# Differential attention on one Trainium2 core: component scores as three terms on two row halves, row sums later, first-token values by split parts

## The chip, the cores and the metric

The program runs on one NeuronCore of one Trainium2 chip. The metric is the device time in microseconds of one execution. The engines are TensorE (PE, with its weight loads shown as PEld), VectorE (DVE), ScalarE (ACT), GpSimd (POOL) and SyncE (SP), which issues most of the DMAs. PSUM holds eight banks of 512 fp32 columns per partition.

## The reference

A streaming encoder block for 2048 tokens behind 16 first ("meta") tokens, model width 1024. One projection feeds two groups of heads side by side: four heads of differential attention and four of latent attention. Their outputs are mixed, normed, added, and a squared-ReLU MLP follows. The change is in the differential attention:

```python
q1, q2 = q[..., 0, :], q[..., 1, :]          # two components of 64 per head
k1, k2 = k[..., 0, :], k[..., 1, :]
s1 = einsum('bhqd,bhkd->bhqk', q1b, k1) * scale + bias   # bias: distance, chunk mask
s2 = einsum('bhqd,bhkd->bhqk', q2b, k2) * scale + bias
a = softmax(s1) - lam * softmax(s2)
return einsum('bhqk,bhkv->bhqv', a, v)       # v: 128 per head
```

## The kernel before

The kernel runs in stages: entry norm and projections, an upward projection of the latent heads (`mla_up`), differential attention (`attention`), latent attention, mixing, MLP. All engines run their own instruction streams and wait for each other on semaphores. The stage of the change begins with the first score matmul of head 0, and the latent attention's first score matmul follows its end on TensorE, in program order.

**Numbers.** TensorE's single-pass fp32r products are made exact enough by parts: each q and k is stored as a high part and a low part (`scr.qk_hi`, `scr.qk_lo`). Before, the q tile of one component stacks 64 rows of high parts on 64 rows of low parts, and the key tile holds [high; high] and [low; low]. Two matmuls over 128 partitions then give all four terms of a component's scores. The value products (`da_ps_o<-da_pT,da_v`) are plain fp32, each run as two instructions.

**Rows.** A head has 16 row tiles of 128 queries (i = 0 to 15). Row tile i sees 16 + 128(i+1) keys, cut by `row_chunks(i)` into 1 to 5 chunks of up to 512 columns: 44 chunks for a head and component, 17,664 columns, so 88 chunks a head. For each chunk TensorE writes scores to one of four PSUM banks (`da_ps_s`). VectorE (L1535) adds the bias, writes to SBUF and takes the chunk's maximum. After the last chunk of a component it makes the row's negated maximum (L1542). ScalarE does the exponentials with their sum (L1481), the first component in `da_rows`, the second in `da_second`. VectorE inverts the sums (L1567, L1574) and weighs the second with lambda (L1576); GpSimd scales the first component (L1473). VectorE's `end` (L1580) adds the second to the first.

**Turning and products.** Four row tiles make a group g. When its four rows have their sums, TensorE transposes the probabilities tile by tile (`turn`, L1646) into three banks (`da_ps_t`); ScalarE copies each to `da_pT` (L1494). `product` (L1660) multiplies it by the value tile into `da_ps_o`. Tile t = 0 belongs to the first tokens: it transposes the first 128 keys, and `v_meta` has zeros but for 16 rows. Group g has 1 + 4(g+1) tiles, so a head has 44, four of them for first tokens.

**Order.** All engines walk one list, `STEPS`, made by `head_steps` for a steady head. `row_steps` lists the chunks and, some chunks later, each row's `exp`, `scale` and `end`. `PHASES` says which groups' rows go with which groups' turns and products: rows of groups 0 and 1 with the previous head's group 3, rows of group 2 with groups 0 and 1, rows of group 3 with group 2. A phase's third figure says how late in it the turns begin, the fourth how many last steps (products and an `out`) are put off into the next phase. `walk` runs the list for each head; a step marked with `back` 1 belongs to the head before. After the last head, its group 3 and the put-off steps run alone. In head 0, TensorE also makes 12 late products of six matmuls for the latent heads (`late_product`, L1629).

**Loads.** SP loads keys and bias one head ahead, q group by group, values when the previous head has used them.

Of the kernel before, what the change touches and what calls it, by code (L numbers as in the profile page):

```python
# [30 lines left out]
P = 128  # L31
# [1075 lines left out]
def by_component(src, h, cols):  # L1107

    return src[ds(h, 1), :, cols].rearrange("a (c p) n -> p (a c) n", c=2)


def load_q(sp, scr, ahead, h, g):
    for j, src in enumerate((scr.qk_hi, scr.qk_lo)):
        sp.dma_start(f32(ahead.q[64 * j:64 * j + 64, g % 2]),
                     by_component(src, h, slice(META + 512 * g, META + 512 * g + 512))).then_inc(ahead.q_loaded[g % 2], 16)


def load_first_keys(sp, scr, ahead, g):

    c0, n = KEY_PIECES[g]  # L1120
    cols = slice(c0, c0 + n)
    for j, src in enumerate((scr.qk_hi, scr.qk_lo)):
        for half in range(2):
            sp.dma_start(f32(ahead.keys[half * 64:half * 64 + 64, j::2, cols]),
                         by_component(src, DA_H, cols)).then_inc(ahead.start_loaded[g], 16)
# [41 lines left out]
def attention(nc, io, scr, ident, ahead, latent):  # L1167
# [8 lines left out]
    with ExitStack() as ctx:  # L1176
        mem = Memory(nc, ctx, io.used)
        keys = (ahead.keys, mem.sb("da_keys", [P, 4, LP], F32R)[:, :, 0:L])
# [5 lines left out]
        NPT = 8  # L1184
        NTB = 3
        pT = mem.sb(f"da_pT", [P, NPT, 512])
        mx = mem.sb("da_mx", [P, 2, COMPS, 5])
        nmax = mem.sb("da_nmax", [P, 2, COMPS])
        nmax_all = mem.sb("da_nmax_all", [P, 5])
        total = mem.sb("da_total", [P, 2, COMPS])  # L1190
        inv = mem.sb("da_inv", [P, 2, COMPS])
        inv2 = mem.sb("da_inv2", [P, 2])
        lam = mem.sb("da_lam", [P, 4])
        v_meta = mem.sb("da_v_meta", [P, P])
        NSB = 4
# [12 lines left out]
        inv2_step = mem.sem("da_inv2_step")  # L1208
# [9 lines left out]
        chunks = [(i, c, k0, n) for i in range(NT) for c in range(COMPS) for k0, n in row_chunks(i)]  # L1218
# [4 lines left out]
        KEY_LOADS = 4  # L1223
# [9 lines left out]

        def comp_row(i, c, u):
            return row(i, u) if c == 0 else second[:, i % 2, 0:META + P * (i + 1)]

        def row_steps(carried):
# [4 lines left out]
            for groups, *_ in PHASES:  # L1242
                steps = []
                for n, (i, c, k0, w) in enumerate(chunks):
# [6 lines left out]
                    if k0 + w == META + P * (i + 1):  # L1251

                        steps += [step for _, step in later if step[2] - NT * step[1] < i]
                        later = [(left, step) for left, step in later if step[2] - NT * step[1] >= i]
                        later.append((1, ("exp", 0, i, c)))
                        if c == 0:
                            later.append((SCALE_AFTER, ("scale", 0, i)))
                        if c == COMPS - 1:
                            later.append((END_AFTER, ("end", 0, i)))
                phases.append(steps)  # L1260
            return phases, [(left, (step[0], 1) + step[2:]) for left, step in later]

# [4 lines left out]
        def cost(step):  # L1267

            if step[0] == "chunk":
                return chunks[step[2]][3] + 60  # L1270
            return META + P * (step[2] + 1) + 250 if step[0] == "end" else 0

        def head_steps():
# [4 lines left out]
            for p, rows_part in enumerate(row_steps(row_steps([])[1])[0]):  # L1278
# [39 lines left out]
        PHASES = (((0, 1), ((1, 3),), 0.2, 7), ((2,), ((0, 0), (0, 1)), 0.15, 7), ((3,), ((0, 2),), 0.2, 7))  # L1318
        SCALE_AFTER, END_AFTER = 2, 5
# [30 lines left out]
        def slot_free(engine, h, n):  # L1350

            if n >= NPT:
                engine.wait_ge(pv_done, NKT * h + n - NPT + 1)
            elif not (isinstance(h, int) and h == 0):
                engine.wait_ge(pv_done, NKT * (h - 1) + last_user(n, NPT) + 1)
# [8 lines left out]
        def _(sp):  # L1364
            def load_keys(h, u):

                for j, src in enumerate((scr.qk_hi, scr.qk_lo)):
                    for half in range(2):
# [2120 lines left out]
```

## Time and profile before

| | us |
|---|---|
| median of 3 runs | 2591.54 (2589.82 to 2594.27) |
| profiled execution | 2589.82 |
| its span, first to last instruction | 2588.0 |
| differential attention in it | 427.0 to 795.5, 368.5 long |

The profile is of one execution. "Busy" of TensorE counts matmuls whose ends are modelled and which overlap, so the distance from one start to the next says what a matmul costs in a row of them. Times in rows are from the span's start.

### The profile page before, as it was taken

What the parts mean: (1) busy time and instruction counts of PE and PEld (TensorE: products, weight loads), DVE (VectorE), ACT (ScalarE), POOL (GpSimd) and SP (SyncE); (2) the same over time, 40 slices, a digit from 0 to 9 for tenths busy, and PEclk for the clock granted to TensorE, in tenths of its full rate; (3) what the DMA queues carried; (4) which work ended last, traced back from release to release, by engine and by line L of the source; (5) the groups of instructions that cost most, each with busy time, mean ns of one, the idle gap of its engine ahead of it and who ended that gap; (6) DMA issues with size and microseconds to landing.
All of it is one profiled execution on the core that took longest, in us unless ns stands there. A gap on an engine that the chain in (4) does not pass through costs nothing.

```text
span 2588.0 us, 35257 instructions
## 1 busy us (share of the span) xinstructions
PE 2526.3 (98%) x12140; PEld 2103.8 (81%) x12140; DVE 1619.0 (63%) x3515; ACT 1211.9 (47%) x2183; POOL 333.4 (13%) x368
## 2 busy tenths in 40 slices
PE   8999999999999999989999999999999999999998
PEld 7998887677667989868877888888888888888886
DVE  6123307998995777754468777867757465564765
ACT  6112314777765565554544333533335353443554
POOL 2110002222221222110000000000000001121133
PEclk9999999999999999999999999999999999999999
DMA  6324458553333111145677666666655365776787
GB/s 225 131 100 132 119 164 263 139 136 94 88 134 92 34 30 46 42 130 163 195 240 224 208 221 214 220 193 210 189 165 175 118 216 106 174 166 161 201 165 139
DMA packets 328956, 398.35 MB, mean 154 GB/s; under 512 B 20896, under 2 KB 235184, under 8 KB 320464
## 3 DMA queue, kind: packets, MB, share of 16 engines
q1 hardware_dynamic: 311216, 364.17, 44.8%
q0 software_dynamic: 17568, 31.99, 8.5%
q8 instruction: 95, 1.56, 0.3%
q14 instruction: 77, 0.63, 0.1%
HBM read 239.62 MB, written 156.48 MB: 153 GB/s over the span
## 4 chain that ended last, share of the span: by engine, by line
PE 62%; DVE 3%; DMA 1%; ACT 1%; issue 1%; SPq 0%; POOL 0%; DVEq 0%; ACTq 0%; POOLq 0%
PE ff_ps_x L3277 26%; PE ff_ps_m L3277 13%; PE ff_ps_z L3277 6%; PE ml_ps_s L2153 6%; PE ff_ps_m L1702 4%; PE ml_ps_o L2184 3%; PE ml_ps_t L2166 2%; DMA ml_v_raw<-scr_yT 1%; DMA ff_pieces<-scr_acc 0%; PE ff_ps_r L2714 0%; PE mo_ps_t L2731 0%; SPq L2341 0%; PE ml_ps_o L2180 0%; DVE ff_pieces L2444 0%; DMA work<-scr_w_vo 0%
## 5 line engine op out<-in xcount | busy, mean ns | idle before, releaser
L3277 PE MATMUL ff_ps_x<-ff_mv_hi_p,ff_st_hi_p 128*128 128x512 f32 x764 | 297.8, 390 | 0.5 <-ACT ff_u L3017 0.5
L3277 PE MATMUL ff_ps_x<-ff_mv_lo_p,ff_st_hi_p 128*128 128x512 f32 x764 | 297.3, 389 | 0.0
L3277 PE MATMUL ff_ps_x<-ff_mv_hi_p,ff_st_lo_p 128*128 128x512 f32 x764 | 297.2, 389 | 0.0
L2153 PE MATMUL ml_ps_s<-wide,ml_qs 128*128 128x416 f32 (+14 forms) x880 | 197.0, 358 | 3.0 <-PEq L137 2.8
L3123 DVE TENSOR_TENSOR ff_st_lo_p<-ff_ps_m,ff_st_hi_p 128x512 fp32r<-128x512 f32 x190 | 130.5, 688 | 103.4 <-ACT ff_st_hi_p L3000 103.4
L2967 POOL DMA_DIRECT2D scr_acc<-ff_pieces x64 | 55.5, 872 | 1015.3 <-DVE ff_pieces L3147 946.8
L3017 ACT ACTIVATE ff_u<-ff_ps_x 128x512 f32<-128x512 f32 x128 | 76.6, 598 | 214.9 <-PE ff_ps_x L3277 214.9
L3277 PEld LDWEIGHTS ff_ps_x<-ff_mv_hi_p,ff_st_hi_p 128*128 128x128 f32 x764 | 143.4, 188 | 32.4 <-issue 2.0
L3277 PEld LDWEIGHTS ff_ps_x<-ff_mv_hi_p,ff_st_lo_p 128*128 128x128 f32 x764 | 143.4, 188 | 29.9
L3277 PEld LDWEIGHTS ff_ps_x<-ff_mv_lo_p,ff_st_hi_p 128*128 128x128 f32 x764 | 143.4, 188 | 29.5
L2153 PEld LDWEIGHTS ml_ps_s<-wide,ml_qs 128*128 128x128 f32 x880 | 153.4, 193 | 15.3 <-issue 3.4
L3000 ACT ACTIVATE ff_st_hi_p<-st_raw 128x512 fp32r<-128x512 f32 x191 | 119.4, 626 | 86.3 <-PE ff_ps_z L3277 86.3
L3277 PE MATMUL ff_ps_m<-wide,ff_st_hi_p 128*128 128x512 f32 x512 | 157.7, 389 | 0.4 <-DVE ff_st_lo_p L2618 0.4
L3000 ACT ACTIVATE ff_st_hi_p<-ff_ps_m 128x512 fp32r<-128x512 f32 x190 | 113.2, 598 | 93.7 <-PE ff_ps_m L3277 93.7
L3277 PE MATMUL ff_ps_x<-wide,ff_st_hi_p 128*128 128x512 f32 x504 | 155.1, 389 | 0.0
L3123 DVE TENSOR_TENSOR ff_st_lo_p<-st_raw,ff_st_hi_p 128x512 fp32r<-128x512 f32 x191 | 130.8, 687 | 36.9 <-ACT ff_st_hi_p L3000 35.6
L2062 DVE CUSTOM_DVE_ANT_0 ml_rows<-ml_ps_s,ahead_bias 128x416 f32<-128x416 f32 (+14 forms) x176 | 100.1, 569 | 67.8 <-PE ml_ps_s L2153 59.8
L1660 PE MATMUL da_ps_o<-da_pT,da_v 128*128 128x512 f32 (+3 forms) x320 | 137.2, 529 | 0.0
L1985 ACT ACTIVATE ml_pT_hi<-ml_ps_t 128x512 fp32r<-128x512 f32 (+3 forms) x176 | 90.6, 537 | 88.6 <-PE ml_ps_t L2166 88.5
L1613 PE MATMUL da_ps_s<-da_keys,ahead_q 128*128 128x416 f32 (+14 forms) x352 | 112.6, 423 | 2.4 <-DVE da_mx L1535 2.4
L3277 PEld LDWEIGHTS ff_ps_m<-wide,ff_st_hi_p 128*128 128x128 f32 x512 | 96.0, 188 | 20.5 <-issue 0.6
L3277 PEld LDWEIGHTS ff_ps_x<-wide,ff_st_hi_p 128*128 128x128 f32 x504 | 94.6, 188 | 19.6
(322 smaller groups left out, 6326.1 us busy)
## 6 DMA issues: line engine op xcount, KB each, us to landing
st_raw<-in_w_ff SPq DMA_DIRECT2D x64, 512.0 KB, 6.1
scr_hid<-ff_pieces SPq DMA_DIRECT2D x128, 256.0 KB, 2.7
st_raw<-scr_hid SPq DMA_DIRECT2D x64, 512.0 KB, 5.6
ring<-in_w_ff SPq DMA_DIRECT2D x28, 1024.0 KB, 8.0
scr_t<-ring SPq DMA_DIRECT2D x24, 1024.0 KB, 6.0
ring<-scr_t SPq DMA_DIRECT2D x21, 1024.0 KB, 8.4
scr_acc<-ff_pieces POOLq DMA_DIRECT2D x64, 256.0 KB, 4.1
ring<-scr_u SPq DMA_DIRECT2D x13, 1024.0 KB, 8.0
```

The source lines that it names most:

```text
L1613: m = pe.matmul(ps_s[n % NSB][:, 0:w], qs[:, g % 2, c, P * b:P * b + P], keys[u][:, 2 * c + j, k0:k0 + w], start=j == 0, stop=j == 1)
L1660: pe.matmul(ps_o[:, c0:512], v_meta[:, :] if t == 0 else v[:, t - 1], pT[0:rows_of, n % NPT, c0:512], start=t == 0, stop=t == tiles_of(g) ...
L1702: m = pe.matmul(bank, y[a][:, k], w[b][:, cols], start=k == 0 and i == 0, stop=k == KD - 1 and i == 2, skip_group_check=True)
L1985: act.activation(pT_hi[0:rows_of, n % NPT, c0:512], ps_t[n % NTB][0:rows_of, c0:512], ACT.Copy).then_inc(hi_copied, 1)
L2062: dve.tensor_tensor_reduce(out=row(i, u)[:, k0:k0 + w], in0=ps_s[n % NSB][:, 0:w], in1=bias[:, b0:b0 + w], scale=1.0, scalar=LOWEST, op0=A ...
L2153: m = pe.matmul(ps_s[n % NSB][:, 0:w], q, k, start=j == 0, stop=j == len(pairs) - 1)
L2184: m = pe.matmul(ps_o[:, c0:512], v[0:rows_of, t - 1], p, start=False, stop=t == tiles_of(g) - 1 and j == 2)
L2967: pool.dma_start(piece_place(scr.acc, name, n), piece[name][u], accum_op=ALU.add).then_inc(added[name][u], 16)
L3000: act.activation(st_hi[kind][:, :, :], stationary(kind, n % 2), ACT.Copy).then_inc(st_hi_ready, 1)
L3017: act.activation(tile, bank[:, :], ACT.Copy).then_inc(taken, 1)
L3123: dve.tensor_tensor(st_lo[kind][:, :, :], stationary(kind, n % 2), f32(st_hi[kind][:, :, :]), ALU.subtract).then_inc(st_lo_ready, 1)
L3277: m = pe.matmul(bank[:, :], w[kind][:, k], a[kind][:, k], start=start and k == 0 and i == 0, stop=stop and k == KH - 1 and i == 2, skip_gr ...
```

## The change

Each component's 64 rows now lie on one half of the partitions: component 0 on 0 to 63, component 1 on 64 to 127, the high and low parts in separate tiles. Scores are three terms (high x high, high x low, low x high). Both components of a chunk are made together, six matmuls on 64 rows into two banks, and the list of chunks alternates the components. VectorE takes minima of negated, scaled values (so no scaling step is left), and one reduction, `most`, finishes both components of a row. The small steps behind a row are separate steps of the list (`row_end`), later than before, with eight slots instead of two; a third place holds second components. More products are put off (ten last steps instead of seven), with eleven `pT` slots instead of eight. For the first tokens' tile, ScalarE rounds the transposed probabilities and the values to fp32r, VectorE puts the remainders of 32 rows beside them on partitions 32 to 63 (`split_meta`, listed after the group's second turn), and two fp32r matmuls replace one fp32 product; TensorE's fourth turn of a group waits for the split. Keys load as two DMAs instead of four.

```diff
 def load_q(sp, scr, ahead, h, g):
     for j, src in enumerate((scr.qk_hi, scr.qk_lo)):
-        sp.dma_start(f32(ahead.q[64 * j:64 * j + 64, g % 2]),
-                     by_component(src, h, slice(META + 512 * g, META + 512 * g + 512))).then_inc(ahead.q_loaded[g % 2], 16)
+        sp.dma_start(f32(ahead.q[:, g % 2, j]),
+                     flat(src[ds(h, 1), :, META + 512 * g:META + 512 * g + 512])).then_inc(ahead.q_loaded[g % 2], 16)
...
-        chunks = [(i, c, k0, n) for i in range(NT) for c in range(COMPS) for k0, n in row_chunks(i)]
+        chunks = [(i, c, k0, n) for i in range(NT) for k0, n in row_chunks(i) for c in range(COMPS)]
...
+        def row_end(i):
+            n = len(row_chunks(i))
+            scale, invert = {NT - 1: (5, 10), 0: (4, 10), 1: (4, 9), 2: (4, 8)}.get(i) or (n + 2, 2 * n + 2)
+            return (("most", 1), ("exp", 1, 0), ("exp", 1, 1), ("scale", scale),
+                    ("invert", invert), ("weigh", invert + 1), ("end", invert + 2))
...
+                    if turn[3] == 1:
+                        body_steps.append(("split_meta",) + turn[1:3])
...
-        PHASES = (((0, 1), ((1, 3),), 0.2, 7), ((2,), ((0, 0), (0, 1)), 0.15, 7), ((3,), ((0, 2),), 0.2, 7))
-        SCALE_AFTER, END_AFTER = 2, 5
+        PHASES = (((0, 1), ((1, 3),), 0.35, 10), ((2,), ((0, 0), (0, 1)), 0.2, 10), ((3,), ((0, 2),), 0.3, 10))
...
             def load_v_meta(h):
-                sp.dma_start(v_meta[0:META, :], scr.v[0:META, ds(h * P, P)]).then_inc(v_loaded[0], 16)
+                for part in range(2):
+                    sp.dma_start(v_meta[32 * part:32 * part + META, :], scr.v[0:META, ds(h * P, P)]).then_inc(v_loaded[0], 16)
...
+                    act.activation(v_meta_parts[:, 0], v_meta[:, :], ACT.Copy).then_inc(v_meta_hi_ready, 1)
...
-                                         in1=bias[u][:, b0:b0 + w], scale=1.0, scalar=LOWEST,
-                                         op0=ALU.add, op1=ALU.max,
...
-                    dve.tensor_scalar(nmax_all[:, 0:nth + 1], mx[:, i % 2, c, 0:nth + 1], -scale, None, ALU.mult, ALU.min,
-                                      accum_out=nmax[:, i % 2, c:c + 1]).then_inc(max_ready, 1)
+                                         in1=bias[u][:, b0:b0 + w], scale=-scale, scalar=-LOWEST,
+                                         op0=ALU.add, op1=ALU.min,
...
+            def most(h, i, **at):
+                last = max(n for n, chunk in enumerate(chunks) if chunk[0] == i)
+                dve.wait_ge(scores_read, NCH * h + last + 1)
+                dve.tensor_reduce(nmax[:, i % NR8, :], mx[:, i % 4, :, 0:len(row_chunks(i))], AX.X, ALU.min).then_inc(max_ready, 1)
...
+            def split_meta(h, g, **at):
+                n = kt_base[g]
+                if g == 0:
+                    dve.wait_ge(v_meta_hi_ready, h + 1)
+                    dve.tensor_tensor(v_meta_parts[:, 1], v_meta[:, :], f32(v_meta_parts[:, 0]), ALU.subtract)
+                dve.wait_ge(copied, NKT * h + n + 1)
+                to = pT_meta
+                dve.tensor_tensor(to[32:64, :], ps_t[n % NTB][0:32, :], f32(to[0:32, :]), ALU.subtract).then_inc(meta_split, 1)
...
-                for j in range(2):
-                    m = pe.matmul(ps_s[n % NSB][:, 0:w], qs[:, g % 2, c, P * b:P * b + P], keys[u][:, 2 * c + j, k0:k0 + w],
-                                  start=j == 0, stop=j == 1)
-                m.then_inc(scores_ready, 1)
+                if c == 0:
+                    if not (isinstance(h, int) and h == 0 and n + 1 < NSB):
+
+                        pe.wait_ge(scores_read, NCH * h + n + 1 - NSB + 1)
+                    for j, (of_q, of_k) in enumerate(((0, 0), (0, 1), (1, 0))):
+                        for comp in range(COMPS):
+                            half = slice(64 * comp, 64 * comp + 64)
+                            m = pe.matmul(ps_s[(n + comp) % NSB][:, 0:w], qs[half, g % 2, of_q, P * b:P * b + P],
+                                          keys[u][half, of_k, k0:k0 + w], start=j == 0, stop=j == 2)
+                            if j == 2:
+                                m.then_inc(scores_ready, 1)
...
+                if t == NTB:
+                    pe.wait_ge(meta_split, NG * h + g + 1)
...
+                if t == 0:
+                    pe.wait_ge(meta_split, NG * h + g + 1)
+                    for part in range(2):
+                        m = pe.matmul(ps_o[:, :], v_meta_parts[:, part], pT_meta, start=part == 0, stop=False)
+                    m.then_inc(pv_done, 1)
+                    return
```

## Rows read from the trace of the kernel before

**Rows 1.** The page: busy time, share of the span and instructions by engine.

```profile
PE 2526.3 (98%) x12140; PEld 2103.8 (81%) x12140; DVE 1619.0 (63%) x3515; ACT 1211.9 (47%) x2183; POOL 333.4 (13%) x368
```

**Rows 2.** Windows: length, busy of PE, PEld, DVE, ACT, POOL; clock, DMA.

```profile
427.00:506.30 79.30, 76.70 (x383) 60.26 (x381) 75.03 (x302) 58.80 (x106) 18.29 (x17) 1.00 0.71 187
506.30:592.70 86.40, 83.45 (x417) 61.37 (x417) 78.38 (x305) 63.16 (x112) 19.01 (x16) 1.00 0.47 111
...
765.30:795.50 30.20, 24.68 (x110) 14.94 (x110) 8.94 (x22) 12.16 (x21) 2.15 (x2) 0.99 0.28 78
```

**Rows 3.** Timeline of TensorE in the projection: start, us, engine, line, operation.

```profile
219.46 0.36 PE L707 MATMUL cv_ps<-cv_w_lo,u_hi 128*128 128x448 f32 x1
219.66 0.37 PE L707 MATMUL cv_ps<-cv_w_hi,u_lo 128*128 128x448 f32 x1
```

**Rows 4.** Groups by line, 427 to 795.5: count, busy us, mean ns, idle before.

```profile
L1660 PE MATMUL da_ps_o<-da_pT,da_v 128*128 128x512 f32 (+3 forms) x320 | 137.2, 529 | 0.0
...
L1646 PE MATMUL da_ps_t<-ident,da_rows 128*128 128x128 f32 x608 | 90.3, 273 | 6.5 <-DVE da_rows L1580 6.5
```

**Rows 5.** Timeline of weight loads in the tail, fp32 products.

```profile
788.30 0.19 PEld L1660 LDWEIGHTS da_ps_o<-da_pT,da_v 128*128 128x128 f32 x1 [0.24 <-issue]
```

**Rows 6.** Waits in head 1 (506.3 to 592.7): waiter, releaser, total us, times, longest.

```profile
PEld da_ps_s L1613 <- DVE da_mx L1535: 4.5, 13, 1.1
...
PEld da_ps_t L1646 <- DVE da_rows L1580: 1.6, 1, 1.6
```

**Rows 7.** VectorE's groups by line in head 1 (506.3 to 592.7).

```profile
L1535 DVE CUSTOM_DVE_ANT_0 da_rows<-da_ps_s,da_bias 128x416 f32<-128x416 f32 (+14 forms) x44 | 23.5, 573 | 2.0 <-PE da_ps_s L1613 1.8
L1535 DVE CUSTOM_DVE_ANT_0 da_second<-da_ps_s,da_bias 128x416 f32<-128x416 f32 (+14 forms) x42 | 22.7, 568 | 0.6 <-PE da_ps_s L1613 0.6
L1580 DVE SCALAR_TENSOR_TENSOR da_rows<-da_second,da_inv,da_rows 128x2064 f32<-128x2064 f32 (+15 forms) x16 | 21.9, 1368 | 1.3 <-POOL da_rows L1473 0.8
...
L1542 DVE TENSOR_SCALAR_CACHE_REDUCE da_nmax_all<-da_mx 128x2 f32<-128x2 f32 (+4 forms) x32 | 5.0, 156 | 1.1
L1576 DVE TENSOR_SCALAR da_inv<-da_inv,da_lam 128x1 f32<-128x1 f32 x16 | 3.4, 214 | 0.6
...
L1567 DVE RECIPROCAL da_inv<-da_total 128x1 f32<-128x1 f32 x16 | 2.6, 161 | 0.8 <-ACT da_rows L1481 0.8
L1574 DVE RECIPROCAL da_inv<-da_total 128x1 f32<-128x1 f32 x16 | 2.5, 157 | 1.6 <-ACT da_second L1481 1.5
```

**Rows 8.** Timeline of weight loads around a 16-row and a 128-row transpose, in the projection.

```profile
219.47 0.19 PEld L707 LDWEIGHTS cv_ps<-cv_w_hi,u_lo 128*128 128x128 f32 x1
219.96 0.32 PEld L721 LDWEIGHTS cv_pt<-ident,o_hi 16*128 16x128 f32 x4 [0.31 <-issue]
...
224.87 0.19 PEld L707 LDWEIGHTS cv_ps<-cv_w_hi,u_lo 128*128 128x128 f32 x1
225.07 0.56 PEld L721 LDWEIGHTS cv_pt<-ident,o_hi 128*128 128x128 f32 x4
```

**Rows 9.** Timeline of all engines in the tail, behind the last row.

```profile
767.27 2.02 ACT L1481 ACTIVATE da_second<-da_second,da_nmax 128x2064 f32<-128x2064 f32 x1 [2.64 <-DVE da_nmax_all L1542]
...
769.86 2.37 DVE L1580 SCALAR_TENSOR_TENSOR da_rows<-da_second,da_inv,da_rows 128x2064 f32<-128x2064 f32 x1
...
772.29 1.53 PE L1646 MATMUL da_ps_t<-ident,da_rows 128*128 128x128 f32 x12 [2.78 <-DVE da_rows L1580]
773.04 1.08 ACT L1494 ACTIVATE da_pT<-da_ps_t 128x512 f32<-128x512 f32 x2 [2.90 <-PE da_ps_t L1646]
...
773.78 0.69 DVE L1594 TENSOR_TENSOR ml_qs<-ahead_q,ml_qs 64x512 fp32r<-64x512 f32 x1
```

**Rows 10.** Timeline of weight loads of 128-column fp32r products, before the stage.

```profile
400.00 0.19 PEld L989 LDWEIGHTS mu_ps<-mu_turned_hi 128*128 128x128 f32 x1
400.11 0.19 PEld L989 LDWEIGHTS mu_ps<-mu_turned_lo,mu_turned_hi 128*128 128x128 f32 x1
```

**Rows 11.** Timeline of weight loads where the weights go from 128 columns to 16.

```profile
209.88 0.09 PEld L707 LDWEIGHTS cv_ps<-w_hi,u_hi 128*16 128x16 f32 x1
```

More of the change, by code:

```diff
@@ L1122, in load_first_keys @@
     for j, src in enumerate((scr.qk_hi, scr.qk_lo)):
-        for half in range(2):
-            sp.dma_start(f32(ahead.keys[half * 64:half * 64 + 64, j::2, cols]),
-                         by_component(src, DA_H, cols)).then_inc(ahead.start_loaded[g], 16)
+        sp.dma_start(f32(ahead.keys[:, j, cols]), src[DA_H, :, cols]).then_inc(ahead.start_loaded[g], 16)
 def load_first_head(sp, io, scr, ahead, g):
@@ L1232, in row, with turned, pT_of @@
             return rows[u ^ (g == 2)][:, i % 4, start:start + META + P * (i + 1)]
+        def turned(n):
+            return n - sum(base < n for base in kt_base)
+        def pT_of(n):
+            at = turned(n) % NPT
+            return pT[:, at] if at < NPT - NPT_MORE else pT_more[:, at - NPT + NPT_MORE]
         def comp_row(i, c, u):
-            return row(i, u) if c == 0 else second[:, i % 2, 0:META + P * (i + 1)]
+            if c == 0:
+                return row(i, u)
+            at, start = (1, sum(META + P * (a + 1) for a in range(i))) if i < 5 else (i % 3, 0)
+            return (third if at == 2 else second[:, at])[:, start:start + META + P * (i + 1)]
         def row_steps(carried):
@@ L1250, in row_steps @@
                     later = [(left, step) for left, step in later if left > 0]
[L1251 to L1259, printed above, removed]
+                    if c == COMPS - 1 and k0 + w == META + P * (i + 1):
+                        later += [(left, (kind, 0, i, *at)) for kind, left, *at in row_end(i)]
                 phases.append(steps)
             return phases, [(left, (step[0], 1) + step[2:]) for left, step in later]
+        def row_end(i):
[3 more added lines that the diff above has]
+                    ("invert", invert), ("weigh", invert + 1), ("end", invert + 2))
         def first_chunk(i):
@@ L1270, in cost @@
                 return chunks[step[2]][3] + 60
-            return META + P * (step[2] + 1) + 250 if step[0] == "end" else 0
+            return META + P * (step[2] + 1) + 100 if step[0] == "end" else 0
         def head_steps():
@@ L1350, in slot_free @@
         def slot_free(engine, h, n):
-            if n >= NPT:
-                engine.wait_ge(pv_done, NKT * h + n - NPT + 1)
+            users = kt_base if n in kt_base else [a for a in range(NKT) if a not in kt_base and turned(a) % NPT == turned(n) % NPT]
+            if n > users[0]:
+                engine.wait_ge(pv_done, NKT * h + users[users.index(n) - 1] + 1)
             elif not (isinstance(h, int) and h == 0):
-                engine.wait_ge(pv_done, NKT * (h - 1) + last_user(n, NPT) + 1)
+                engine.wait_ge(pv_done, NKT * (h - 1) + users[-1] + 1)
         late_banks = ps_t + [ps_o]
```

88 lines of the change are left out of this document (46 added, 42 removed).

## The prediction

> **What bounds the kernel now.** Read first the page's busy shares [rows 1]: TensorE is busy 98% of the span, so time goes only where TensorE has less to do or waits less. The change touches the differential attention alone, so next the busy times by stretch [rows 2]. Its boundaries are the first score matmul of each head and of the next stage: a first head of 79.3 us, three heads of 86.4, 86.4 and 86.2, a tail of 30.2, together 368.5 us at a granted clock of 1.00 (the 2.4 GHz level; 0.99 in the tail). In a full head VectorE is nearly as busy as TensorE, 78.4 against 83.5 us. Busy TensorE is not TensorE at its peak, so I count what each engine needs by itself.
>
> TensorE, per head. The score chunks of `row_chunks` hold 17,664 columns; two components and two matmuls stream them four times. Matmuls of 448 columns start 0.20 us apart [rows 3], 0.445 ns a column, so 4 x 17,664 x 0.445 = 31.4 us. Transposes: 608 in four heads, 152 a head [rows 4], 0.11 us each (twelve take 1.53 us [rows 9], one alone 0.27 [rows 4], so eleven steps of 0.115): 16.7 us. Value products are two fp32 instructions each, 320 for 160 products [rows 4], whose weight loads (0.19) come after 0.24 idle [rows 5], so 0.43 us apart: 0.86 us for 512 columns, 17,408 columns a head, 29.2 us. The products of the 16 first tokens: four of 0.86, 3.4 us. Sum **80.7 us of 86.4**. The missing 5.7 are waits for VectorE: 4.5 for a score bank, 1.6 for a finished row, in the loads' rows [rows 6].
>
> VectorE, per head. Of its idle time, waits for another engine are 1.8 + 0.6 + 0.8 + 0.8 + 1.5 = 5.5 us [rows 7]. So it needs **80.9 us** with its own short stalls. The two engines are equal; whichever the change makes longer sets the head.
>
> **TensorE after the change.** *Scores.* For each chunk both components run together: three terms, each a matmul on partitions 0 to 63 and one on 64 to 127, six in all. The trace holds no matmul on 64 rows. If the halves stream side by side and nothing else counts, 3 x 17,664 x 0.445 = 23.6 us. From the other side, each of the six needs its own weight load of 128 columns; such loads, where the matmul is short, follow each other 0.11 us apart [rows 10]. Six in a row leave the last matmul starting 5 x 0.11 after the first: 44 x 0.55 + 17,664 x 0.445 = 32.1 us. A pair of 416 columns would take 0.74 against 0.74 now. I take 28, the middle: loads of the other half may hide in part. Term: -3.4 (-7.8 to +0.7).
>
> *Entering and leaving the half-row form.* Within one form the next weights load while a matmul runs: the loads of four transposes start at 225.07, 0.20 after the products' last load, at the products' own pace [rows 8]. The same step at 219.96, where the operand has 16 rows, idles 0.31 us, put down to "issue": nothing was waited for [rows 8]. The last product had started at 219.66 [rows 3] and streamed 0.20, so the array ran dry. Such small transposes alone could not fill it: their four loads take 0.32, against 0.56 for the full-size ones. It is the trace's only change of row form between busy stretches. A change of column form (16 weight columns at 209.88) loads with no idle time [rows 11], so it is the rows that cost. In the new order of steps nearly every pair of score chunks stands between transposes or products in the 128-row form: from the listed order, 43 separate excursions a head for 44 pairs. At 0.31 each, 13.3 us. Bounds: nothing, if 64 rows behave unlike 16, and 13.3. I take 13.3, the nearest row.
>
> The Trainium skill, "TensorEngine Tiling (Array Packing)", Key Properties, says that changing the tiling mode drains TensorE while moving between tiles of one mode does not. The 0.31 us agrees; the undelayed change of column form does not, so the rule holds here at most for rows. By it the sum is the one just made. The skill's "TensorE: Matmul & The Clock Gate", Part 3 on packing small matmuls, reports tiles of different rows starting about 4 ns apart; no run here shows it, and by it the scores would cost 23.6 and not 28.
>
> *First tokens.* Four fp32 products of 0.86 become eight of 512 columns at 0.23: -1.6 us.
>
> Sum: 80.7 - 3.4 + 13.3 - 1.6 = **89.0 us** (84.6 to 93.1; without the excursions 71.3 to 79.8).
>
> **VectorE after.** Removed: 32 small maxima, 5.0 us and 1.1 idle, and the stalls between inverse, weight and sum, 0.6 + 0.5 [rows 7]. Added: 16 reductions over both components; between nothing seen (hidden under the chunk before) and the 214 ns of the weighting I take 0.156, the small reduction they replace, 2.5 us (0 to 3.4); four splits of the first tokens at 0.69 (the 64-row subtraction, [rows 9]) and one of 128 columns at about 0.3, 3.1 us. Net -1.6: 79.3 us. The sum of each row moves later by chunks, so its waits on ScalarE (1.5 + 0.8) and GpSimd (0.8) go. But the splits wait in VectorE's queue: in the listed order three of four stand directly after a row's sum or after two exponentials queued on ScalarE, with the transposes and ScalarE's copy still to come. From the end of a sum at 772.23 to the end of the first copy (773.04 plus half of 1.08) is 1.4 us [rows 9], so 4.2 us a head, in which the next score chunks queue behind the split and TensorE's fourth transpose group waits too. Together **83.5 us**, under TensorE's 89.0. ScalarE gains one small copy a head at 63 of 86 us busy [rows 2]; GpSimd keeps its work.
>
> **DMAs.** Keys come as two loads instead of four with half the bytes, a head ahead; the q loads keep theirs; the first tokens' values load twice, 16 rows each. SP issues one fewer a head in sum, and no wait for keys, q or values stands among the waits [rows 6]: nothing gained or lost; had a load been late, it would take the place of VectorE's 4.5 us.
>
> **The stage.** Full head: TensorE's 89.0 plus waits; VectorE now has room, so of 5.7 I keep 3: 92.0, +5.6 over 86.4, three times 16.8. Bounds 84.6 + 3 and 93.1 + 5.7: +1.2 to +12.4 each.
> First head: it lacks the last head's third-group work and carries 12 late products of six matmuls at 0.23 (16.4): TensorE needs 31.4 + 16.4 + 29.2 for its transposes and products, less 5.1 put off to the next head, 72 of 79.3; VectorE, with hardly a wait, sets it. After: some 38 excursions add 11.8, scores -3.4, first tokens -1.2, three more products put off -2.6: 77. VectorE's 79.3 less 1.6 and one split less, plus two splits' waits of 1.4: 80. I take +1 (-3 to +4).
> Tail: the ten last steps instead of seven are put off, three products at 0.86, +2.6; the first-token product -0.4. Row 15's two exponentials (2.0 each, [rows 9]) now follow its last chunk, ahead of its sum, behind nine products of 0.86. +2.1.
> Later stages are unchanged and start later: 16.8 + 1 + 2.1 = **+20 us**. The profiled execution took 2589.82 us (span 2588.0), 1.7 under the median of 2591.54; +20 on the median gives **2611 us**, 2594 to 2636 by the bounds.
>
> **Rivals.**
> 1. *No charge for the half-row form.* For it: one excursion in the whole trace carries the charge, and on 16 rows. Then TensorE needs at most 79.8 and VectorE sets the head: 83.5, or 81.4 if half of the splits' waits hide, plus 1: -2 to -4 a head, the first about -1, the tail +2.1: 2583 (2573 with no split waiting, to 2589). It decides when an excursion costs under some 0.1 us.
> 2. *The halves don't stream side by side.* Six passes: 47.2 us of scores, TensorE at 94.9 without and 108.2 with excursions, plus 3: +11.5 to +25 a head, +5 to +16 in the first: 2633 to 2685. Against it: separate partitions and banks; no row for or against.
> 3. *It breaks even.* An excursion at 0.1 leaves TensorE near 80 and VectorE with the splits' waits near 83.5 with waits both ways: 2587 to 2597.
>
> **Chances.** My forecast 0.45, no charge 0.36, serial halves 0.07, break-even 0.12. What a measurement can tell from no change is about 0.2%, 5.2 us. Slower by more: nearly all of the forecast and the serial case, 0.50; faster by more: nearly all of rival 1, 0.35; within: 0.15. The signs are both open, so the range runs from rival 1 to the forecast's upper bounds, **2576 to 2630**, leaving out the serial case and both far ends; the forecast's own range is 2597 to 2630.
>
> **What the changed profile would show.** Right: full heads of about 92 us; "issue" idle ahead of weight loads on both sides of each 64-row group, about 0.3 together; VectorE idle more than now, waiting for scores; the small maxima gone, splits of 0.69 with waits ahead of them. Rival 1: 64-row loads without idle time and heads of 82 to 85 with VectorE over 95% busy. Rival 2: the two halves' matmuls start a whole matmul apart, 0.18 us or more at 416 columns, not 0.11 or less. The tail says whether the later sums cost 2 us. I am wrong above all if 64 rows change form for free.

## The result, and the profile after

The change makes the kernel slower: 2654.11 us median (2651.46 to 2656.28, 4 runs) against 2590.68 (2588.25 to 2594.27, 4 runs) on the same chip, ratio 1.0243 with a 95% interval of 1.0225 to 1.0261. I had forecast slower, by +20 us; it is +63, beyond the range's end at 2630.

The page after, the busy line that answers to [rows 1]: TensorE's busy time rises by 40 us, VectorE's falls by 12.

```profile
PE 2566.2 (97%) x12492; PEld 2077.9 (78%) x12492; DVE 1607.3 (61%) x3343; ACT 1208.5 (46%) x2187; POOL 334.2 (13%) x368
```

Windows after, with the same boundaries as [rows 2]: the first head, a full head, the tail (length, busy of PE, PEld, DVE, ACT, POOL, clock, DMA share, GB/s).

```profile
428.50:518.20 89.70, 82.17 (x463) 51.44 (x464) 69.47 (x255) 55.78 (x105) 16.34 (x15) 0.94 0.36 127
518.20:620.60 102.40, 93.11 (x508) 54.90 (x506) 75.13 (x261) 62.49 (x113) 18.95 (x17) 0.95 0.21 73
...
825.40:858.00 32.60, 27.13 (x119) 16.17 (x115) 11.49 (x21) 13.83 (x23) 2.86 (x3) 1.00 0.25 73
```

The first head grows by 10.4, the full heads by 16.0, 16.0 and 16.2, the tail by 2.4: 61.0 of the span's 66.5. The stage starts 1.5 later, and the stages behind it, with the same instructions, take 1796.5 instead of 1792.5 (clock 0.99 instead of 1.00). The clock column is new: in full heads it was 1.00, now 0.95. Behind it are whole stretches at half rate (0.5, the 1.2 GHz level), 3.4 and 6.8 us long, 10.2 us of each full head. Here are the two of one head, and the window behind the second, at full rate again:

```profile
533.40:536.80 3.40, 3.40 (x17) 2.67 (x16) 1.40 (x6) 1.79 (x3) 0.00 (x0) 0.51 0.07 26
598.30:605.10 6.80, 6.37 (x28) 4.64 (x28) 2.87 (x10) 2.29 (x5) 1.27 (x1) 0.50 0.00 0
605.10:610.00 4.90, 4.90 (x34) 3.06 (x32) 3.99 (x16) 3.37 (x4) 0.39 (x1) 1.00 0.00 0
```

The waits of that head (waiter, releaser, total us, times, longest) answer to [rows 6]. Now both engines wait for each other: VectorE 21.8 us for scores, TensorE 7.8 for banks and over 6 for two finished rows.

```profile
DVE da_rows L1551 <- PE da_ps_s L1644: 21.8, 24, 2.9
...
PEld da_ps_s L1644 <- DVE da_mx L1551: 7.8, 17, 0.8
...
PEld da_ps_t L1680 <- DVE da_rows L1608: 6.5, 2, 3.4
...
DVE da_pT_meta L1602 <- ACT da_pT_meta L1510: 4.2, 3, 1.9
```

The weight loads around one pair of chunks (start, duration, idle before). Products' loads follow each other every 0.43; the first half-row load starts 0.95 after the last of them, when the array has run dry. The next product's load starts 0.76 after the first half-row load, where three terms of 416 columns at 0.445 ns stream 0.56: dry again. (e17 below gives the price of both sides.)

```profile
559.23 0.19 PEld L1700 LDWEIGHTS da_ps_o<-da_pT,da_v 128*128 128x128 f32 x1 [0.24 <-issue]
560.18 0.49 PEld L1644 LDWEIGHTS da_ps_s<-da_keys,ahead_q 64*128 64x128 f32 x6 [0.76 <-issue]
560.94 0.30 PEld L1700 LDWEIGHTS da_ps_o<-da_pT,da_v 128*128 128x128 f32 x2 [0.28 <-issue]
```

Several engines at one group's end in the same head. TensorE idles 2.9 us for the last row's sum (L1608), the clock is at half by the time that its transposes begin, and ScalarE, the split, and the score chunk behind the split come one after another.

```profile
596.84 1.83 DVE L1608 SCALAR_TENSOR_TENSOR da_rows<-da_third,da_inv,da_rows 128x1552 f32<-128x1552 f32 x1
...
598.73 1.97 PE L1680 MATMUL da_ps_t<-ident,da_rows 128*128 128x128 f32 x8 [2.89 <-DVE da_rows L1608]
599.94 0.60 ACT L1510 ACTIVATE da_pT_meta<-da_ps_t 128x512 fp32r<-128x512 f32 x1 [1.14 <-PE da_ps_t L1680]
600.57 0.68 DVE L1602 TENSOR_TENSOR da_pT_meta<-da_ps_t,da_pT_meta 32x512 fp32r<-32x512 f32 x1 [1.90 <-ACT da_pT_meta L1510]
...
602.34 0.66 DVE L1551 CUSTOM_DVE_ANT_0 da_rows<-da_ps_s,da_bias 128x480 f32<-128x480 f32 x1 [1.09 <-PE da_ps_s L1644]
```

So two theories. **A**: the half-row form costs it, with its 43 excursions a head. **B**: the new order of work costs it, with no half rows needed. The runs say how much each.

### The profile page after: what moved, and what is told of

Same layout as the page of the kernel before. It is cut to its first block, busy times and chain, and to the rows that moved or that the text cites. A ratio compares the mean times of both kernels' runs of the same rounds, so it can differ in the third digit from the quotient of the medians.

```text
span 2654.5 us, 35807 instructions
## 1 busy us (share of the span) xinstructions
PE 2566.2 (97%) x12492; PEld 2077.9 (78%) x12492; DVE 1607.3 (61%) x3343; ACT 1208.5 (46%) x2187; POOL 334.2 (13%) x368
## 4 chain that ended last, share of the span: by engine, by line
PE 60%; DVE 3%; DMA 2%; ACT 1%; issue 1%; SPq 0%; POOL 0%; DVEq 0%; ACTq 0%; POOLq 0%
PE ff_ps_x L3317 25%; PE ff_ps_m L3317 13%; PE ff_ps_z L3317 6%; PE ml_ps_s L2193 6%; PE ff_ps_m L1742 4%; PE ml_ps_o L2224 3%; PE ml_ps_t L2206 2%; DMA ml_v_raw<-scr_yT 1%; DMA ff_pieces<-scr_acc 0%; PE ff_ps_r L2754 0%; PE mo_ps_t L2771 0%; SPq L2381 0%; PE ml_ps_o L2220 0%; DVE ff_pieces L2484 0%; DMA work<-scr_w_vo 0%
## 5 line engine op out<-in xcount | busy, mean ns | idle before, releaser
L1680 PEld LDWEIGHTS da_ps_t<-ident,da_rows 128*128 128x128 f32 x608 | 76.2, 152 | 76.2 <-issue 28.6
L1680 PE MATMUL da_ps_t<-ident,da_rows 128*128 128x128 f32 x608 | 100.5, 300 | 32.9 <-DVE da_rows L1608 23.3
L2025 ACT ACTIVATE ml_pT_hi<-ml_ps_t 128x512 fp32r<-128x512 f32 (+3 forms) x176 | 90.6, 537 | 88.6 <-PE ml_ps_t L2206 88.5
L1484 POOL TENSOR_SCALAR da_rows<-da_rows,da_inv 128x144 f32<-128x144 f32 (+7 forms) x64 | 75.9, 1187 | 328.1 <-DVE da_inv L1583 328.1
L1492 ACT ACTIVATE da_rows<-da_rows,da_nmax 128x144 f32<-128x144 f32 (+7 forms) x64 | 77.7, 1213 | 84.7 <-DVE da_nmax L1561 84.4
```

Of the source, the lines that this page charges most:

```text
L1484: pool.tensor_scalar(row(i, u), row(i, u), inv[:, i % NR8, 0:1], 1.0, ALU.mult, ALU.mult).then_inc(first_scaled, 1)
L1492: act.activation(comp_row(i, c, u), comp_row(i, c, u), ACT.Exp, bias=nmax[:, i % NR8, c:c + 1], scale=-1.0, accum_out=total[:, i % NR8, c: ...
L1680: m = pe.transpose(ps_t[n % NTB][0:rows_of, P * b:P * b + P], row(4 * g + b, u)[:, k0:k0 + rows_of], ident[:, :])
L2025: act.activation(pT_hi[0:rows_of, n % NPT, c0:512], ps_t[n % NTB][0:rows_of, c0:512], ACT.Copy).then_inc(hi_copied, 1)
```

## The experiments

All ratios are to runs of the kernel before on the same chip (medians 2589.1 to 2592.0), with 95% intervals.

### With and without half rows, in the new order

**e1, three full-row matmuls for a pair of chunks; e2, four; e3, e4, one small matmul more.**

```
-  six matmuls on qs[half], keys[u][half], side by side
+  for comp, terms in enumerate((((0, 0), (0, 1)), ((1, 0),))):      # e1; e2: two terms in each
+      m = pe.matmul(ps_s[(n + comp) % NSB], qs[:, g % 2, of_q, ...], keys[u][:, of_k, ...])
# e3 (rows = 64), e4 (rows = 128): e1, and ahead of each pair
+  pe.matmul(ps_s[n % NSB][:, 0:16], qs[0:rows, g % 2, 0, ...], keys[u][0:rows, 0, k0:k0 + 16], start=True, stop=True)
```

> The kernel after, with the six half-row score matmuls of a pair of chunks replaced by three matmuls on all 128 rows (two into the first component's bank, one into the second's): the scores mix the components and lack terms, everything else (order of steps, pair-wise bank waits, later sums, splits) is as after. Theory A (the half-row form costs it: about 0.4 us of TensorE at 43 excursions a head, and the waits and half-clock stretches that follow): TensorE needs 80.7 - 31.4 + 23.6 - 1.6 = 71 us a head, VectorE about 77 plus 4 of split waits sets it, heads of 81 to 85, 2575 to 2592 us in all, no half-clock stretch in the heads. Theory B (the new order costs it: sums too late, TensorE waiting for banks by pairs and for rows, splits in VectorE's queue): heads stay above 94, 2620 us or more.

2610.07 us, ratio 1.0082 (1.0065 to 1.0099). Between the theories: 44 us come back, 20 don't, though TensorE has 7.8 us less to do a head than before.

> As the run with three, but four matmuls on 128 rows for a pair of chunks, two into each bank, which is the TensorE work of the kernel before in the order of the kernel after (scores mix the components). Theory A: TensorE needs 79 us, VectorE 77 plus 4 of split waits, both near the bound: heads of 84 to 88, 2583 to 2597 us. Theory B: above 2625 us. The distance from the run with three tells what 7.8 us of plain streaming a head is worth in this order.

2616.29 us, 1.0106 (1.009 to 1.0123): with before's TensorE work, the new order alone costs some 27 us. The 7.8 us of streaming a head between e1 and e2 are worth 6 us in all.

> The run with three, plus one matmul on partitions 0 to 63 of 16 columns ahead of each pair of chunks, written over by the pair. Its streaming is next to nothing (16 columns, 0.007 us), so what it adds is 43 changes of row form and back a head. Theory A: 43 x 0.4 to 0.5 = 17 to 21 us of TensorE on 71, so 88 to 93 needed a head and heads of 93 to 103: 2615 to 2655 us, with half-clock stretches back. Theory B, or changes of form that are free: within 8 us of the run with three.

2649.26 us, 1.0228 (1.0211 to 1.0245).

> The control to the run before: the same 16-column matmul ahead of each pair, on all 128 rows, so no change of form. Both theories: 43 more loads of at most 0.11 us, under 5 us of TensorE a head where it has room: within 6 us of the run with three. If it is as slow as its half-row twin, it is the additional instruction and not the form that costs.

2619.93 us, 1.0118 (1.0101 to 1.0135). The twins differ by 29 us, in nothing but the row form of 176 tiny matmuls (44 pairs in each of four heads): that is theory A's, at 0.17 us each in an order where TensorE has time to spare. e4 is 4 us beyond what I had allowed an instruction without a change of form.

A full head of e1, two of e2 and one of e3, windows: e1 at clock 0.94 and e2 at 1.00 take the same time, and in none is TensorE or VectorE busy throughout. The two heads of e2 have the same steps and the same idle stretches ahead of their sums' transposes (3.10 and 2.66 us), but in the first the clock falls behind each of them, for 3.4 us (from 521.8 and 583.2), and in the second it does not. The first is 2.7 us longer: 0.4 for each us at half rate.

```profile
599.00:691.20 92.20, 78.94 (x374) 57.83 (x374) 74.44 (x261) 61.99 (x113) 19.08 (x17) 0.94 0.23 81
```

```profile
507.80:602.90 95.10, 85.34 (x417) 64.68 (x417) 74.76 (x262) 62.13 (x113) 19.05 (x17) 0.96 0.23 79
602.90:695.30 92.40, 82.53 (x419) 61.93 (x418) 74.50 (x262) 61.94 (x113) 19.09 (x17) 1.00 0.23 81
```

```profile
519.10:621.30 102.20, 93.95 (x417) 64.01 (x416) 75.31 (x261) 62.50 (x113) 18.96 (x17) 0.97 0.21 73
```

### What in the order costs it: first guesses

**e5** takes the splits out of after, **e6** gives it before's list, **e7** both, **e8** both with four full-row matmuls.

```
# e5, e7, e8
-  body_steps.append(("split_meta",) + turn[1:3])
-  two matmuls of v_meta_parts[:, part] with pT_meta, behind meta_split
+  pe.matmul(ps_o[:, :], v_meta[:, :], f32(pT_meta[:, :]), start=True, stop=False)
# e6, e7, e8
+  PHASES as before;  scale, invert = 3, 4      # so "end" stands at 6
```

> The kernel after with the first tokens' values as one fp32 product again: no split on VectorE, no rounding of the values on ScalarE, no wait of TensorE's fourth turn for the split; half-row scores and order as after. The run with three full-row matmuls took 20 us more than the kernel before with TensorE needing only 71 us a head, so the order itself costs some 20 to 26 us. Theory S (the splits in VectorE's queue are most of that): VectorE loses 3.1 us of splits and 4 to 5 us of waits a head against 1.6 more for TensorE: 12 to 20 us faster than after, 2634 to 2642. Theory P (the list of steps: later sums, bunched put-off products): within 6 us of after, 2648 to 2660.

2667.18 us, 1.0291 (1.0274 to 1.0308): 13 us slower than after. Both theories miss. The splits save TensorE 1.6 us a head by my sum, 6 of the 13; the full heads also have 10.2 to 13.7 us at half rate, against 10.2 after. What the rest is, no run shows.

> The kernel after with the list of steps of the kernel before: the three figures of the phases and seven put-off steps as before, and each row's sum six chunks behind its last chunk (scale at 3, invert 4, weigh 5, end 6). Splits and half-row scores stay. Theory P: 15 to 25 us faster than after, 2629 to 2639. Theory S: within 6 us of after; slower by more than that if the later sums did hide waits on ScalarE's exponentials.

2654.24 us, 1.0242 (1.0225 to 1.0259): no change, so theory P falls by itself as S did.

> Both of the edits before together, so that of the change the half-row scores, the alternated components with their banks by pairs, and VectorE's small steps are left. If the list and the splits are all that the order costs, and the half-row form the rest (29 us by the runs with one small matmul, 44 by the run with three): 2619 to 2636 us. If the pair-wise banks or the half rows cost more than that, it stays above 2640.

2650.21 us, 1.0226 (1.0209 to 1.0243): above 2640, so list and splits together don't hold it either.

> The run before with four matmuls on 128 rows for a pair of chunks instead of six on half rows (scores mix the components): the TensorE work of the kernel before, with the alternated components, banks by pairs, and VectorE's cheaper small steps. If nothing but half rows, list and splits costs: 2578 to 2592 us, as the kernel before or a little faster, since VectorE has some 4 us less a head. If the pairs of components are a cost of their own: above 2600.

2631.62 us, 1.0157 (1.014 to 1.0174): worse than e2, which had the late list and the splits. The guess that these two are the order's cost falls; before's list doesn't suit pairs whose exponentials both come at the row's end. In e8's trace VectorE waits for exponentials ahead of its inverses, three such lines of 5.2, 4.6 and 2.5 us between 500 and 595; with the late list of after such waits are all but gone (0.2 us in a head of e1). So the late list seems to answer to the joint exponentials; e8 differs from e2 in the splits too, and no run parts the two.

### One edit at a time, with full rows

From e2 back to before: **e9** single banks, **e10** the components one after the other, **e11** a maximum and exponential for each component, **e13** before's list, **e14** no splits. (e12, e15, e16 are below.)

```
# e9    -  pe.wait_ge(scores_read, NCH * h + n + 1 - NSB + 1)    # both banks, ahead of the pair
#       +  pe.wait_ge(scores_read, NCH * h + n - NSB + 1)        # own bank, at the chunk's own place
# e10   +  chunks = [... for i in range(NT) for c in range(COMPS) for k0, n in row_chunks(i)]
# e11   +  later += [(1, ("most", 0, i, c)), (1, ("exp", 0, i, c))]    # behind each component
# e13   +  PHASES as before; scale, invert = 3, 4
# e14   +  the first tokens' product in fp32, no split
```

> The run with four full-row matmuls in the order of the kernel after (2616 us, 26 over the kernel before; scores mix the components), but each chunk's two matmuls stand at their own place in the list and wait for their own bank alone, as in the kernel before; components still alternate. Theory W (a pair needs two of the four banks free at once, so TensorE and VectorE run in lockstep): most of the 26 us comes back, 2590 to 2602. Theory L (both exponentials wait for the row's joint last chunk, so sums, turns and splits come late): within 6 us of 2616.

> The run by single banks, with all chunks of the first component ahead of those of the second, as in the kernel before; the joint maximum and both exponentials still come behind the row's last chunk (scores mix the components). Theory W: as the run by single banks, within 5 us. Theory L: the same within 5 us too, since the exponentials come no sooner; only if the alternation of the components is a cost of its own does it gain, 5 to 15 us.

> The sequential run with a maximum for each component as soon as it is read, and its exponential right behind, as in the kernel before (32 small reductions a head on VectorE again, 16 more than the run before, 2.4 us; scores mix the components). Theory L: the first component's exponential starts half a row sooner, 8 to 20 us faster than the sequential run. Theory W: 0 to 8 us slower than it, by the 2.4 us a head.

> The run with each component's own exponential (full-row matmuls by single banks, 2613 us; scores mix the components), now with the list of the kernel before: phases, seven put-off steps, sums six chunks behind the row. The splits stay. Theory P (with banks and exponentials as before, the late list is what is left): 12 to 22 us faster, 2590 to 2600. Theory S (the splits hold it): within 6 us of 2613. There TensorE waits 6 us a head for two late sums, at 3.3 each, so theory P has a place in the trace.

> The same run with the first tokens' product in fp32 and no splits, so that against the kernel before only VectorE's separate small steps, the joint layout of two components in one tile and the free place in memory are left (scores mix the components). Both theories: 2583 to 2595 us, as the kernel before; if it stays above 2600, something that was taken for free is not.

| run | put back as before, one more in each row | median us | ratio (95%) |
|---|---|---|---|
| e2 | full-row matmuls, four to a pair | 2616.29 | 1.0106 (1.009 to 1.0123) |
| e9 | single banks | 2625.50 | 1.0136 (1.0119 to 1.0153) |
| e10 | components one after the other | 2620.06 | 1.0118 (1.0101 to 1.0135) |
| e11 | own exponentials | 2612.65 | 1.0086 (1.0069 to 1.0103) |
| e13 | before's list | 2602.40 | 1.0055 (1.0039 to 1.0072) |
| e14 | no splits | 2594.23 | 1.0019 (1.0009 to 1.0029) |

By the ratios: theory W falls, single banks are slower than pairs in this order, by 8 us. Own exponentials give back 8, the low end of what theory L expected. Before's list gives 8, between what P and S expected, and the splits another 9. The alternation's 5 is within the intervals. What e14 still costs, 5 us, I can't place: its VectorE steps, its layout of keys and its place in memory differ from before. Together the ladder leads home: the order's 27 us are several small delays, none of them the whole, and each edit's worth holds for its place in this ladder only (e6 and e8 show that).

The clock has a part in these worths. Two full heads of e10 and one of e11 (windows): e10's at full rate is 0.8 us longer than e11's, its next, with 6.8 us at half rate, 3.4. All heads of e11 are at full rate. At the 0.4 us from e2, e10's 17.0 us of half rate in four heads make some 7 (an estimate), so most of what the own exponentials give back is half rate that no longer occurs.

```profile
510.70:603.80 93.10, 82.01 (x418) 61.61 (x417) 75.64 (x261) 62.38 (x113) 19.06 (x17) 1.00 0.23 80
603.80:699.50 95.70, 84.88 (x417) 64.17 (x416) 75.98 (x261) 62.57 (x113) 19.03 (x17) 0.96 0.23 78
```

```profile
600.30:692.60 92.30, 82.49 (x418) 61.54 (x418) 76.37 (x278) 62.92 (x114) 19.11 (x17) 1.00 0.23 81
```

A full head of e14, windows, then lines of its waits, and last those of e2 in a full head:

```profile
592.80:679.80 87.00, 82.97 (x416) 61.81 (x417) 74.23 (x273) 63.01 (x113) 19.04 (x16) 1.00 0.25 86
```

```profile
DVE da_rows L1543 <- PE da_ps_s L1632: 4.5, 9, 1.4
...
DVE da_second L1543 <- PE da_ps_s L1632: 4.1, 9, 1.1
...
PEld da_ps_t L1665 <- DVE da_rows L1600: 3.2, 2, 2.0
...
DVE da_third L1543 <- PE da_ps_s L1632: 2.1, 4, 0.9
```

```profile
DVE da_rows L1551 <- PE da_ps_s L1643: 13.1, 15, 2.7
PEld da_ps_t L1678 <- DVE da_rows L1608: 6.1, 2, 3.3
...
DVE da_pT_meta L1602 <- ACT da_pT_meta L1510: 4.3, 3, 1.5
```

From e2 to e14 TensorE's wait for late rows goes from 6.1 to 3.2 us, VectorE's for the splits from 4.3 to none, and its waits for scores from 13.1 to 10.7 (three lines). The waits overlap in part and don't add up to a time; the head is 5.4 us shorter.

### Fewer excursions

**e12**: two pairs in one excursion. **e15**: its control with full rows (e1, grouped alike). **e16**: e12 with two sums sooner.

```
 def scores(h, n, pair, u):
+    if n % 4 == 0:                       # e15: the same with e1's matmuls
+        for first in (n, n + 2):
+            pair_of_chunks(h, first, pair, u)
# e16: row_end, rows 7 and 11:  scale, invert = 4, 6
```

> The kernel after, with two pairs of chunks made back to back in the half-row form, at the place of the first: 22 excursions a head instead of 43; nothing left out. By the excursions alone: 21 x 0.4 = 8.6 us a head less on TensorE, 34 us over four heads, 2620 to 2635. By theory W: the second pair waits until VectorE has read the pair before, with all work behind it in TensorE's queue held up, which gives the gain back: 2645 to 2700.

2623.30 us, 1.013 (1.0113 to 1.0147): 31 us faster than after, for half the excursions. A full head of e12, windows, has clock 0.98; its loads now come twelve at a time:

```profile
607.50:703.30 95.80, 84.05 (x507) 54.16 (x506) 74.29 (x262) 61.88 (x113) 19.05 (x17) 0.98 0.23 78
```

```profile
576.49 1.12 PEld L1644 LDWEIGHTS da_ps_s<-da_keys,ahead_q 64*128 64x128 f32 x12 [0.76 <-DVE da_mx L1551]
577.91 0.30 PEld L1706 LDWEIGHTS da_ps_o<-da_pT,da_v 128*128 128x128 f32 x2 [0.30 <-issue]
```

> The control to the run with two pairs in one excursion (2623 us, 31 faster than after): the same grouping with three full-row matmuls for a pair, which has no change of form to save (scores mix the components; ungrouped 2610 us). If fewer changes of form made the gain, grouping gains nothing here and costs bank waits: 2605 to 2625. If grouping itself is better for TensorE's order: 2580 to 2595.

2603.67 us, 1.0062 (1.0046 to 1.0079): grouping without a form to change gives 6, so some 25 of e12's 31 are the excursions', 0.30 us for each of 84 saved.

> The run with two pairs in one excursion (2623 us), with the sum of the last row of groups 1 and 2 four and two chunks sooner (scale at 4, end at 8); nothing left out. TensorE waits 5.5 us a head there for two sums, 3.3 at most, and the clock is at half for 3.4 us a head behind one of them. If the late sums hold it: 8 to 20 us faster, 2603 to 2615. If the exponentials and not the place in the list are late: within 5 us of 2623.

2620.66 us, 1.0125 (1.0108 to 1.0142): within 5 us, so the place of those two sums in the list isn't what holds e12. No version beat the kernel before.

### One excursion by itself

**e17, e18**: the kernel before, with a small matmul ahead of each accumulation of the MLP, where TensorE sets the time.

```
 def product(kind, n, bank, start, stop):
+    if start:                            # rows = 64 in e17, 128 in e18
+        pe.matmul(bank[:, 0:16], st_hi[kind][0:rows, 0], mv_hi[kind][0:rows, 0, 0:16], start=True, stop=False, ...)
```

> The kernel before, its attention unchanged, with one 16-column matmul on partitions 0 to 63 ahead of each accumulation of the MLP stage (190 of them, written over by the accumulation), where TensorE runs at its own pace and no other engine sets the time. By the excursion's price as read from the starts of loads and matmuls in the profile after (about 0.2 us on the way in and 0.2 out): 190 x 0.3 to 0.42 = 57 to 80 us over its full-row twin. By the theory that the form is nearly free and the waits around it cost: under 25 us.

2667.33 us, 1.0296 (1.0279 to 1.0313).

> The control: the same 190 matmuls of 16 columns on all 128 rows, so no change of row form. Both theories: 0 to 21 us over the kernel before (at most one load of 0.11 us each).

2617.06 us, 1.0103 (1.0087 to 1.012). The twins differ by 50.3 us: 0.26 us for each of 190 changes of form and back, and against before the detour costs 77.0 / 190 = 0.41. I had compared the whole detour with the twin: the 57 to 80 fits the 77 against before, and 50 falls a little short. The twin itself takes 27, where I had 21 at most. The weight loads of e17, then of e18:

```profile
2000.23 0.19 PEld L3279 LDWEIGHTS ff_ps_z<-ff_mv_hi_p,ff_st_lo_p 128*128 128x128 f32 x1
2000.77 0.18 PEld L3276 LDWEIGHTS ff_ps_x<-ff_mv_hi_p,ff_st_hi_p 64*128 64x128 f32 x1 [0.35 <-issue]
2000.97 0.19 PEld L3279 LDWEIGHTS ff_ps_x<-ff_mv_hi_p,ff_st_hi_p 128*128 128x128 f32 x1
2001.08 0.19 PEld L3279 LDWEIGHTS ff_ps_x<-ff_mv_lo_p,ff_st_hi_p 128*128 128x128 f32 x1
```

```profile
2010.29 0.19 PEld L3279 LDWEIGHTS ff_ps_x<-ff_mv_hi_p,ff_st_lo_p 128*128 128x128 f32 x1
2010.52 0.19 PEld L3276 LDWEIGHTS ff_ps_z<-ff_mv_hi_p,ff_st_hi_p 128*128 128x128 f32 x1
2010.74 0.19 PEld L3279 LDWEIGHTS ff_ps_z<-ff_mv_hi_p,ff_st_hi_p 128*128 128x128 f32 x1
2010.85 0.19 PEld L3279 LDWEIGHTS ff_ps_z<-ff_mv_lo_p,ff_st_hi_p 128*128 128x128 f32 x1
```

From the last load ahead of the detour to the second behind it: 0.85 us with half rows, 0.56 with full rows, 2 x 0.23 where nothing is put in. So 0.39 by the rows, 0.41 by the time. On the way in the half-row load starts 0.54 after the load before, its twin 0.23.

But the way out is charged too, as the starts of single matmuls in the trace of after show at the pair above. The last product ahead streams from 559.66 for 0.43, to 560.09. The second and third terms start at 560.47 and 560.66, 0.19 apart, so the first streamed from 560.29, 0.20 late, and the third to 560.85. The second product behind starts at 561.48, so the first streamed from 561.05, again 0.20 late. In the three full heads the way in is 0.20 (median of 125), and 39 of 41 excursions between two products cost 0.40 to 0.42 in all. In e17 the full-row load on the way out starts only 0.20 after the half-row load because the 16 columns between them stream in next to nothing. The twin pays on that side too, about 0.11 by the starts, since so short a matmul doesn't cover the next load; that is why the twins differ by 0.26 and not by 0.41.

## Why the prediction was right or wrong

**Right: the mechanism and the sign.** A change of row form is charged, as the one row of [rows 8] said: there the load idled 0.31; in e17 it starts 0.31 later than its twin. That row shows the way in alone, and I took it for the whole; the runs charge the way out as well. The Trainium skill, "TensorEngine Tiling (Array Packing)", Key Properties, says that a change of tiling mode drains TensorE, and for rows the trace agrees, at 0.26 to 0.41 us a detour. Rival 1 (no charge) falls with e17, e12 and e3.

**Right in sum by luck, wrong in two terms.** The scores were to cost 28; they cost the lower bound, 23.6. Six half-row matmuls take as long as three full-row ones, here in after (336 columns), then in e1 (352 columns):

```profile
591.52 0.72 PE L1644 MATMUL da_ps_s<-da_keys,ahead_q 64*128 64x336 f32 x6
```

```profile
628.07 0.73 PE L1643 MATMUL da_ps_s<-wide,ahead_q 128*128 128x352 f32 x3
```

The two halves of a term start 3 to 4 ns apart in after (560.180 and 560.183, 560.474 and 560.477, 560.660 and 560.664), so rival 2 falls too. The Trainium skill, "TensorE: Matmul & The Clock Gate", Part 3 on packing small matmuls, has such tiles start about 4 ns apart; the trace agrees. An excursion costs some 0.40, 0.20 on each side, not 0.31: 43 make 17.2 instead of 13.3 (the trace of after has 127 in three heads). TensorE then needs 80.7 - 31.4 + 23.6 + 17.2 - 1.6 = 88.5 us a head; I had 89.0, because 4.4 too much for the scores and 3.9 too little for the excursions nearly cancel. Held against the times: 172 excursions at 0.405 less four times 7.8 of streaming make 38 us, and after stands 38 over e2 (by the ratios, 1.0243 against 1.0106, 35).

**Wrong: "VectorE now has room, so of 5.7 I keep 3".** This step carries most of the miss. The head takes 102.4, so 13.9 us over the need, not 3; in three heads that is 33 us more than I had, and the first head adds 9. e2 shows that they aren't the half rows' doing: with a need of 79.1 for TensorE and less work than before for VectorE, its head at full clock still takes 92.4, 13 us over. I compared the sums of two engines' work and called the difference room. But the change also delays what each hands to the other: both exponentials behind the row's joint end, the list's later sums, and the splits, which I had at 4.2 us of waits a head and which wait 4.2, but as covered by TensorE; taking them out makes 9 us between e13 and e14. I priced what these moves remove from VectorE's queue and left out what they make late for TensorE. The order costs 27 us (e2), where my sum has a gain.

**Missing: a term for the clock.** The profile before shows no half rate in the heads; after has 10.2 us of it in each. It comes at TensorE's idle stretches at a group's end (2.89 us ahead of 598.73, 3.23 ahead of 532.79), but not at each such stretch: one of e2's two heads has the same ones as the other and stays at full rate. At the 0.4 us for each us at half rate that those two heads show, 10.2 us cost some 4 us of a full head (an estimate). So about 4 of the 13.9 are the clock, behind waits, and 10 the waits themselves. It also hides what e1 gains: its head has 10.2 us at half rate and is as long as e2's at full rate, though it needs 7.8 less.

**First head, tail, VectorE.** The first head was to gain 1 and gained 10.4. In e2 it is 81.4 long and gains 2, so some 8 go with the half rows, half of them by the clock (0.94, an estimate as above). My sum had hidden the excursions there under VectorE's 80: again I compared two engines' sums of work and counted no wait between them. The tail: +2.4 for +2.1. VectorE's busy time fell by 3.3 us a head, where my terms make it rise by 0.6 (2.5 + 3.1 - 5.0). The reductions of `most` are 16 of 0.15 us, the splits 0.68 each, as costed, but I had left out the accumulator reads that go with the small maxima, in head 1 of before:

```profile
L1542 DVE DVE_READ_ACCUMULATOR da_nmax_all<-da_mx 128x1 f32 x32 | 2.6, 82 | 0.0
```

They overlap other work, so they explain at most 2.6 of the 3.9. The rest of the span, 4.0 us in unchanged stages and 1.5 at the start, I had not counted. The 1.5 go with a stretch at half rate ahead of the stage (0.50 from 424.2 to 427.6) that before does not have, and the later stages' clock is 0.99 instead of 1.00; why, no run shows. (The prediction's upper bound of 2636 comes to 2635 by its own terms.)

## What to carry to other kernels

Count how often a stream changes the row form of its matmuls before packing them on half rows: here a detour cost 0.40 us and a pair saved 0.18, so two pairs to a detour (e12) only about break even on TensorE. And when two engines hand work to each other every microsecond, a sum of each one's work is a lower bound; what a step that moves later makes late for the other engine needs a price of its own, best tested by a run with the new order and the old work (e2).

## What the runs showed of the hardware

Two half-row matmuls on different partitions cost one full-row matmul's time (six in 0.72 us at 336 columns). A full-row matmul of only 16 columns, put ahead of an accumulation, costs 27 / 190 = 0.14 us, though its columns stream in 0.007. A change of row form costs 0.20 us on the way in and 0.20 on the way out between products (39 of 41 excursions after: 0.40 to 0.42). Two heads of e2 with the same steps differ by 2.7 us for 6.8 us at half rate. And a TensorE with less to do can earn no time: e1 needs 7.8 us a head less than e2, its clock falls to 0.94, and its head is as long as e2's at full rate.
